# Turning all attention probabilities on VectorE in 32 by 32 blocks, with value products over 32 rows

## What is computed

```python
sc = einsum('bqkgd,bckd->bqkgc', qg, kv_c[:, :, 0]) * scale       # compressed blocks: 32 means of 32 keys
pc = masked_softmax(sc, mc);  o_c = einsum('bqkgc,bckd->bqkgd', pc, kv_c[:, :, 1])
...                                                               # top 16 of 16 blocks of 64: all causal keys
ps = masked_softmax(ss, ms);  o_s = einsum('bqkgns,bqknsd->bqkgd', ps, g[..., 1, :])
sw = einsum('bqkgd,blkd->bqkgl', qg, kv_w[:, :, 0]) * scale       # window: the last 512 keys
pw = masked_softmax(sw, mw);  o_w = einsum('bqkgl,blkd->bqkgd', pw, kv_w[:, :, 1])

o = sum(sigmoid(g_raw) * o_br, axis=branches)                     # layer_output
y_att = rms_norm(o * silu(z_a), att_norm_g)
mix = concatenate([y_ssd, y_att]) @ w_out
y = rms_norm(x + gate[:, None] * mix, final_g)
```

## Time and profile before

| what | us |
|---|---|
| median of three runs | 952.32 (951.27 to 952.5) |
| the profiled execution | 953.35 |
| its span, first to last instruction | 951.5 |
| TensorE busy in the span | 903.9 (95%) |
| VectorE, ScalarE, GpSimd busy | 473.2, 361.1, 148.6 |

### The profile page before, as it was taken

One profiled execution on the slowest core, in us unless ns is written; L12 is line 12 of the kernel. 1 busy time (PEld: TensorE's weight loads), 2 busy tenths in 40 slices (PEclk: granted clock), 3 DMA queues, 4 the chain that ended last, 5 costly groups with the idle time before them and its releaser, 6 DMA issues.

```text
span 951.5 us, 13061 instructions
## 1 busy us (share of the span) xinstructions
PE 903.9 (95%) x5085; PEld 546.6 (57%) x5085; DVE 473.2 (50%) x951; ACT 361.1 (38%) x731; POOL 148.6 (16%) x128
## 2 busy tenths in 40 slices
PE   2999999999999999998999997899999999999995
PEld 1454664465566556666455554566766665756752
DVE  1142211055353535448434458877675766658553
ACT  3040000201011244555233347666564655454531
POOL 1002583002000143335111103600000000000000
PEclk9999999999999999999999999899999999999999
DMA  8916335223120000304433304300010110101011
GB/s 295 381 54 271 133 132 207 87 89 134 43 90 1 0 5 1 89 0 156 166 137 137 137 5 154 130 1 23 2 35 1 46 33 12 46 1 45 13 34 66
DMA packets 36567, 80.72 MB, mean 85 GB/s; under 512 B 3044, under 2 KB 17580, under 8 KB 35162
## 3 DMA queue, kind: packets, MB, share of 16 engines
q1 hardware_dynamic: 32010, 49.45, 15.1%
q0 software_dynamic: 4496, 30.44, 8.4%
HBM read 69.70 MB, written 14.30 MB: 88 GB/s over the span
## 4 chain that ended last, share of the span: by engine, by line
PE 89%; DVE 5%; ACT 2%; issue 2%; DMA 1%; SPq 1%; DVEq 0%; ACTq 0%
PE PS L1692 12%; PE PS L1622 12%; PE PS L1965 12%; PE PS L1672 11%; PE PS L2024 7%; PE PS L2001 6%; PE PS L2048 6%; PE PS L1591 3%; PE PS L1781 2%; PE PS L1541 1%; PE PS L1916 1%; DMA W<-in_w_ada 1%; PE PS L1844 1%; PE PS L1626 1%; PE PS L2042 1%
## 5 line engine op out<-in xcount | busy, mean ns | idle before, releaser
L1692 PE MATMUL PS<-hT,W 128*128 128x363 f32 (+1 forms) x384 | 118.6, 469 | 0.0
L1672 PE MATMUL PS<-W,hT 128*128 128x512 f32 x256 | 113.0, 594 | 0.5 <-DVE W L1327 0.5
L1046 ACT ACTIVATE T<-PS,small 128x640 f32<-128x640 f32 (+7 forms) x128 | 88.7, 705 | 46.1 <-DVE small L1482 44.2
L1692 PEld LDWEIGHTS PS<-hT,W 128*128 128x128 f32 x384 | 72.2, 189 | 45.6 <-issue 1.7
L1482 DVE TENSOR_REDUCE small<-PS 128x1 f32<-128x640 f32 (+7 forms) x86 | 82.5, 971 | 28.4 <-PE PS L2015 27.7
L1622 PE MATMUL PS<-W,hT 128*128 128x288 f32 (+1 forms) x256 | 86.5, 500 | 0.0
L2024 PE MATMUL PS<-consts,T 128*128 128x128 f32 x544 | 80.8, 279 | 3.3 <-DVE U L1522 1.6
L2024 PEld LDWEIGHTS PS<-consts,T 128*128 128x128 f32 x544 | 61.9, 142 | 37.7 <-issue 31.0
L1672 PEld LDWEIGHTS PS<-W,hT 128*128 128x128 f32 x256 | 47.9, 190 | 56.3 <-issue 54.8
L1622 PEld LDWEIGHTS PS<-W,hT 128*128 128x128 f32 x256 | 48.5, 190 | 37.4 <-issue 30.7
L1965 PE MATMUL PS<-U,Y 128*128 128x512 f32 x128 | 60.0, 597 | 2.4 <-DVE Q L1502 1.3
(11 more groups left out here) (430 smaller groups left out, 1500.3 us busy)
## 6 DMA issues: line engine op xcount, KB each, us to landing
W<-in_w_in SPq DMA_DIRECT2D x5, 2048.0 KB, 8.6
W<-in_w_ada SPq DMA_DIRECT2D x8, 1024.0 KB, 10.0
U<-in_x_prompt SPq DMA_DIRECT2D x8, 512.0 KB, 7.5
W<-in_w_ada SPq DMA_DIRECT2D x2, 2048.0 KB, 7.8
U<-in_state_win_kv POOLq DMA_DIRECT2D x8, 512.0 KB
hT<-in_x_prompt SPq DMA_DIRECT2D x8, 512.0 KB, 3.9
out_y_prompt<-hT SPq DMA_DIRECT2D x8, 512.0 KB, 3.0
out_new_win_sample<-in_state_win_kv POOLq DMA_DIRECT2D x1, 4032.0 KB, 22.9
```

The costliest lines, as they stand in the source:

```text
L1046: ins = act.activation(Pb[u % 4][:, m * step:m * step + n * P], S[:, m, :], ACT.Exp, bias=sneg_m[u % 2][:, m:m + 1], accum_out=dsum[i % 2] ...
L1672: ins = nc.tensor.matmul(bank(z_bank(u)), hT3[:, k, i * P:(i + 1) * P], w, start=(k == 0), stop=(k == KT8 - 1))
L1692: ins = nc.tensor.matmul(bank(b, 0, n), w[:, k, ct % 4 * P:ct % 4 * P + P], hT3[:, k, a:a + n], start=(k == 0), stop=(k == KT8 - 1))
```

## The change

Probabilities are no longer turned on TensorE. ScalarE writes the exponents of a branch for all eight heads whole, the selected branch's in hT (hT3), the window's in T. VectorE then turns each block of 32 x 32 where it is (nc.vector.transpose, steps TURNP and CT; in the program's list STREAM_TRANSPOSE). After that a partition group of 32 rows, j, holds 32 keys (block b of a key tile) for the 32 queries 32j to 32j + 31. So the products go over 32 rows: for each key tile, block b, group j and KV head one matmul with K = 32 and M = 64, on 4 heads x 32 queries = 128 columns (step PV). Group j writes bank 4 + j, the KV head is the column half. The values must stand in each of the four partition groups: SP loads them four times from DRAM (VREP; v_dram holds the window's), tiles 0 to 4 before the attention, 5 to 7 during it into places that have come free. COPY gathers the four banks. The c branch does the same (CV): 32 matmuls a tile with K = 32 and M = 32, on 64 columns, all in one bank.

Around it the following moves: the banks 4 to 7 are handed out by tables (BANK, FREE, EMPTY), so OUT takes any of them; gate_p is multiplied into w_out by GpSimd (WGATE) once OUT 0 is done, and RES becomes one add; GpSimd takes the adds of BACK, the gate's product of GATE and that with final_g; ScalarE takes the scalings of SCALE and FINAL and all copies of queries; the c branch's mask is a table; the SSD rows of the tiles 2 to 7 are parked in DRAM (y_dram) and fetched again; x rows are loaded once the store from their place has landed. ORDER is written anew.

```diff
+        PROB = {"s": hT3[:, :, 0:SEQ], "w": T[:, 0:5 * 1024].rearrange("p (h s) -> p h s", h=AH)}
+        C = KcTs[:, 0:AH * NCB]
+        VREP = {("s", 0): Vs[:, 0:512], ("s", 1): Vs[:, 512:1024], ("w", 0): Vw[:, 0:512], ("w", 1): Vw[:, 512:1024],
+                ("s", 5): hst[:, :], ("s", 6): cmpm[:, 0:512], ("s", 7): Y3[:, TT, :]}
+        VREP |= {(k, 2 + n // 2): Y3[:, 2 + n, :] for n, k in enumerate("swswsw")}
+        VREP |= {("w", t): VREP["w", t - 5] for t in range(5, TT)}
...
-            "pttpvvvvpvvcorkoogooaruoofoonrohooofrnhf")
+            "scxodxkossdoafxdxuytossdxodxowssdtoxdorxssdodtnxxtossdodxorsxmsgrdxattdxvctftkuvckngoaooooorouooronhoooofofrorn"
...
             for k in (2, 3, 4, 5, 6, 7, 0, 1):
...
                 nc.gpsimd.tensor_scalar(wo[:, k, :], wo[:, k, :], mixgT[:, k:k + 1], None, ALU.mult).then_inc(s_wo_scaled, 1)
+            for what, u in STEPS:
+                if what == "WGATE":
+                    if u == 0:
+                        pool.wait_ge(s_gates_in, 64)
+                        pool.wait_ge(s_out, 2)
+                        pool.wait_ge(s_wo_scaled, 8)
+                    w = wo[:, u, :].rearrange("p (n c) -> p n c", n=4)
+                    nc.gpsimd.tensor_tensor(w, w, gate_p, ALU.mult).then_inc(s_wo_scaled, 1)
+                if what == "BACK":
...
+                    nc.gpsimd.tensor_tensor(Q3[:, i, :], Q3[:, i, :], spare, ALU.add).then_inc(s_added, 1)
+                if what == "GATE" and u:
...
+                    nc.gpsimd.tensor_tensor(Q3[:, tile, :], Q3[:, tile, :], za[tile], ALU.mult).then_inc(s_zmul, 1)
+                if what == "SQUARE":
...
+                    nc.gpsimd.tensor_tensor(x, x, fin_g[0:rows(MIX[u])].rearrange("p (h c) -> p h c", h=2), ALU.mult).then_inc(s_added, 1)
...
+                        if i:
+                            act.wait_ge(s_values, 2 * i - (1 if k == "s" else 0))
...
+                            ins = act.activation(PROB[k][:, hh, 0:n * P], S[:, m, :], ACT.Exp, bias=sneg_m[u % 2][:, m:m + 1],
+                                                 accum_out=dsum[i % 2][:, " sw".index(k), hh:hh + 1])
...
-                    act.activation(OT, bank(6), ACT.Copy).then_inc(s_copied, 1)
+                    act.activation(OT.rearrange("p (g a q) -> p a g q", g=GQ, a=4), PS[:, 4 * 512:].rearrange("p (a s) -> p a s", a=4)[:, :, 0:P]
+                                   .rearrange("p a (g q) -> p a g q", g=GQ), ACT.Copy).then_inc(s_copied, 1)
...
-                    nc.vector.tensor_tensor(x, bank(7) if u else bank(7)[SR * again:SR * again + SR], gate_p[:, c] if u else gate_s[again],
-                                            ALU.mult).then_inc(s_gated, 1)
...
-                    nc.vector.tensor_tensor(x, x, xre[u % 2][0:r, again, :], ALU.add).then_inc(s_summed, 1)
+                        nc.vector.tensor_tensor(x, use_bank("OUT", u, again), x, ALU.add).then_inc(s_summed, 1)
...
+                if what == "TURNP":
+                    us = TURNS[u]
+                    i, k, _, nh = UNITS[us[0]]
+                    n = keys(us[0])[1]
+                    dve.wait_ge(s_exp, us[-1] + 1)
+                    for hs in turn_heads(us):
+                        x = PROB[k][:, hs, 0:n * P]
+                        ins = nc.vector.transpose(x, x)
+                    ins.then_inc(s_pturned, 1)
...
-                    for n, (unit, c) in enumerate(x for b in bl for x in b[3]):
-                        ins = nc.tensor.transpose(bank(4 + F % 2, n * P, (n + 1) * P), Pb[unit % 4][:, c:c + P], ident)
+                elif what == "CV":
+                    pe.wait_ge(s_pturned, TURNED["CT", u])
+                    bank_free("CV", u, 0)
+                    for h in range(AH):
+                        for j in range(4):
+                            q, a = slice(32 * j, 32 * j + 32), h // GQ * 256 + j * HD
+                            ins = nc.tensor.matmul(use_bank("CV", u, 0)[q, h * HD:(h + 1) * HD], C[q, 32 * h:32 * h + 32], Vbd[q, a:a + HD],
+                                                   start=True, stop=True)
+                    ins.then_inc(s_cv, 1)
+                elif what == "PV":
+                    i, k = u // 2, "sw"[u % 2]
+                    a = max(0, i - WIN // P) if k == "w" else 0
+                    pe.wait_ge(s_pturned, TURNED["TURNP", LAST_TURN[i, k]])
+                    if k == "s":
+                        pe.wait_ge(kvin[i % 2], 16 + 16 * 8 * (i // 2 + 1))
+                    bank_free("PV", u, 0)
+                    for t in range(a, i + 1):
+                        for b in range(4):
+                            for j in range(4):
+                                q, c = slice(32 * j, 32 * j + 32), (t - a) * P + 32 * b
+                                for kv in range(KVH):
+                                    ins = nc.tensor.matmul(bank(4 + j, 0, P)[HALF[kv]].rearrange("p (g q) -> p g q", g=GQ),
+                                                           VREP[k, t][q, b * P + kv * HD:b * P + kv * HD + HD],
+                                                           PROB[k][q, kv * GQ:kv * GQ + GQ, c:c + 32],
+                                                           start=(t == a and b == 0), stop=(t == i and b == 3))
                     ins.then_inc(s_values, 1)
...
+            def load_values(t):
...
+                for k, rows_of in (("s", O["new_slc_prompt"][0, 0, t * P:(t + 1) * P, 1].rearrange("s h d -> s (h d)")), ("w", v_dram[t * P:(t + 1) * P])):
+                    for j in range(4):
+                        sp.dma_start(VREP[k, t][32 * j:32 * j + 32].rearrange("p (b c) -> p b c", b=4),
+                                     rows_of.rearrange("(b p) c -> p b c", b=4)).then_inc(kvin[t % 2], 16)
...
             for n, tile in enumerate(MIX):
-                sp.wait_ge(s_squared, n + 1)
+                if 5 <= n + 3 < TT:
+                    sp.wait_ge(s_values, 2 * (n + 2) + 2)
+                    load_values(n + 3)
```

More of the change, by code:

```diff
@@ L133, in constants, with build_layer @@
     return out, np.ascontiguousarray(np.concatenate(list(parts.values()), axis=1).astype(f))
[L136 removed]
+def build_layer(nc, A, O, where, ncols, gate_dram, out_dram, y_dram, v_dram):
     ctx = ExitStack()
@@ L388, in build_layer @@
         gate_rows = Y[0:9, 3328:4352]
+        WLOADS = [sum(len(GROUPS[n]) for n in range(len(GROUPS)) if SLOT[n] == x) for x in range(2)]
         def arrived(eng, g):
@@ L637, in emptying @@
-        def emptying(what, u):
-            return FILLS["T", u] if what == "EMPTY" else FILLS.get((what, u), []) if what != "T" else []
-        def turn_parts(what, u, n):
-            b = bank(4 + emptying(what, u)[n] % 2)
-            if what == "TURN":
-                return [(mixT(MIX[u], n), b[:, 0:4 * rows(MIX[u])])]
-            cols = P * sum(len(bl[3]) for bl in TGROUPS[u][1])
-            return [(PT[u % NPT][:, 0:cols], b[:, 0:cols])]
-        def q_bank(u):
-            return bank(4 + FILLS["QT", u][0] % 2) if u else bank(6)
@@ L654, in build_layer @@
-        xre = [hT3[:, 2 * n:2 * n + 2, 512:1024] for n in range(2)]
-        res = [hT3[:, 4 + 2 * n:6 + 2 * n, 512:1024] for n in range(2)]
-        gate_p, fin_g = W[:, 0:DM], W[:, DM:2 * DM]
+        POS = {(what, u, again): n for n, ((what, u), again) in enumerate(zip(STEPS, AGAIN))}
+        ROOTED = {step: n + 1 for n, step in enumerate(step for step in STEPS if step[0] in ("SCALE", "FINAL"))}
+        ADDED = {step: n + 1 for n, step in enumerate(step for step in STEPS if step[0] in ("BACK", "SQUARE"))}
@@ new lines, in use_bank, with square_junk @@
+        def use_bank(*use):
+            return bank(BANK[use])
+        def q_bank(u):
+            return use_bank("QT", u, 0) if u else bank(6)
+        xrows = [W[:, (1 + n) * DM:(2 + n) * DM] for n in range(2)]
+        xres = [x.rearrange("p (h c) -> p h c", h=2) for x in xrows]
+        gate_p, fin_g = hT3[:, 0:4, 768:1024], W[:, 0:DM]
+        def square_junk(u):
+            return hT3[:, 4:8, 768:1024] if u <= 3 else W[:, 4096 + 512 * (u - 2):5120 + 512 * (u - 2)].rearrange("p (n c) -> p n c", n=4)
```

415 lines of the change are left out of this document (206 added, 209 removed).

## The result

The changed kernel takes 966.0 us (median of four runs, 961.3 to 972.4), against 951.8 for the kernel before: 1.015 of its time, with a 95% interval of 1.009 to 1.022. It is slower, by 14 us, where I had forecast 54 us less. Its runs also lie further apart than those of before (951.1 to 952.5). The profiled execution is 961.28 us, the fastest of the four, and its span is 959.5.

A forecast was written before the change was run, and what follows sets the result against it. From OUT 0 on TensorE was taken as the bound: 611.5 to OUT 0, 251.5 of TensorE work, 18 for VectorE, 3 for GpSimd, 4 for value loads and 9.3 of tail made a span of 897.3; forecast 898 us, range 874 to 955.

The forecast's parts named there:

- The values: Value products on TensorE behind OUT 0: eight tiles at once, 13.6 ns a record, 56.6 us for 57.7, 1.1 off.
- The transposes: TensorE's turns of probabilities: all 544 records go, 70.3 us off behind OUT 0.
- OUT 0: Stretch before OUT 0: it begins at 611.5 us instead of 616.3, 4.8 off, held by the scaling of w_out.
- VectorE: VectorE's work from 568 us on becomes 225 us; TensorE waits 18 us for it, from 5 to 40.
- GpSimd's w_out product: GpSimd multiplies gate_p into w_out behind OUT 0, 18.8 us; OUT 1 waits 3 us, from 0 to 8.
- Value loads: SP's fetches of values for tiles 5 to 7 during attention: 4 us of waiting, from 0 to 12.
- The tail: Work after the last matmul: 9.3 us for 8.0, from 7.5 to 10.5.
- (1): Value products: only four tiles run at once, 27 ns a record; 942 us, from 930 to 955; chance 0.14.
- (3): VectorE's transposes take two passes, 72 us more, and VectorE bounds the phase; 925 us; chance 0.10.
- (4): The c products, four row groups writing one bank, run one after another, 27 us for 7; 918 us; chance 0.05.
- (2): TensorE's instructions come too slowly for the products; gain used up at 14.7 ns each, 996 us at 20; chance 0.15.

The follow-up runs named there:

- The experiment: The kernel before, with each transpose of probabilities made twice, 544 records more: 1006.6 us, 54.0 more.
- quarter_values: The changed kernel with only the first 32 keys of each key tile in the value products, 528 matmuls for 2112: 909.6 us.
- early_adds: The changed kernel with the two adds of BACK of tile 0 made by VectorE again, not GpSimd: 954.8 us, 1.0004 of before.
- one_head: The changed kernel with most 32-row products on one head's 32 columns instead of four heads' 128, same number of instructions: 989.1 us.
- merged37: early_adds with some 40% of the 32-row products of both KV heads merged, in branches of three and more key tiles: 963.5 us.
- merged_first_a: early_adds with merged products for both KV heads, all of a branch's merged ones first and then the others: 953.3 us.

## Why the prediction was wrong

The sum was 897.3 us for the span, and the profiled span is 959.5. Of the 62 us, 15 lie before OUT 0 and 48 behind it; the tail gives 1 back. (The median of the runs lies 5 us above the profiled one.)

**The values.** The pace was right: 14 ns a record, eight tiles at once. The rule of 25 ns between starts of the Trainium skill ("TensorE: Matmul & The Clock Gate", Part 1, "Wait — 56ns, not 53.3ns?") doesn't hold between different tiles here, by the same 14 ns. What failed is that I made the supply of instructions a rival that decides all or nothing, with a break-even at 14.7 ns an instruction and 0.15 for it, and put it at nothing in the sum. It was there at 13.5 to 14.6 ns (256 in 3.45 to 3.73 us), half as fast as the products ask: 29 us of idle time behind OUT 0, and some 6 us more in the streams. The rival's own formula would have said so: at 13.5 ns it gives 898 + 57 - 13 = 942. I worked out a packet each 1.7 us from the earlier trace rows, and had no row that said a packet could come that often.

**The transposes.** This term was mis-sized: I took 70.3 us off, and 56.7 went, since the busy time of a group isn't its share of the time. The experiment gave 99 ns a record, where I took 145; by it only 48 us went. The same that I used for the pace of 0.43 us had the time from start to start: eight turns begin at 884.36 and the next work at 885.32, 120 ns each.

**OUT 0.** It began at 626.3 us, 14.8 later than the 611.5 of the sum. The step said that nothing else before 616.3 changes on TensorE's path. I had GpSimd's new adds down as "covered by OUT and scores" and priced them, but didn't place them in GpSimd's queue, where the order shows them behind L848 (the rows L848, L865 stand in the section on the change). So I priced the adds and missed that the first ones stand behind 23 us of other work.

**VectorE.** The transposes in blocks took what the nearest row said, 128 x 2048 in 2293 ns, and VectorE's whole work from 568 us on was 231.9 us, where I had 225.

```profile
L1550 DVE STREAM_TRANSPOSE hT<-hT 128x2048 f32<-128x2048 f32 x4 | 9.2, 2293 | 0.0
```

The shortage was over-sized: I had 18 us for it, and all waits for other engines behind OUT 0 rose by 12. I take it that the slower TensorE gave VectorE time. With the still shorter products of quarter_values the waits for ScalarE's exponents rose by 14 us; what they would be with all products at full pace no run shows.

**GpSimd's w_out product** took 2485 ns each, for 2350 in L705's row, and TensorE did not stand still for it, where I had put 3 us. **Value loads** cost nothing visible, where I had put 4 us. **The tail** is 8.7 us, near the 9.3 of the sum.

**The rivals.** (1), four tiles at once, and (3), two passes, are out. (4) is out: a tile's c products span 1.0 us, though four row groups write one bank.

```profile
879.05 1.10 PE L2069 MATMUL PS<-Vbd,KcTs 32*32 32x64 f32 x64
880.07 0.53 PE L2048 MATMUL PS<-KTw,W 64*128 64x320 f32 x1
```

The Trainium skill ("TensorEngine Tiling (Array Packing)", Gotcha 1) says that different row tiles can't access the same PSUM bank at one time. The trace doesn't agree: the 64 records take 16 ns each with the array's depth, where one after another they would take 53. (2) was the right mechanism with a wrong size, and alone it wouldn't have made the kernel slower: without GpSimd's queue the change is a draw. In the long run the draw has a simple sum, an estimate from these rows. A key tile costs 128 instructions, 1.73 us at 13.5 ns each. Before, it cost 8 turns of 99 ns and 16 records of 56 ns, 1.69 us.

**Still open:** why a fetch starts some 1 us after a resumption and is usable 1.3 to 1.6 us after it has landed; why scores between the products made the kernel slower; and the spread of the runs (961 to 972 us). The mean clock of its four runs is 0.972 to 0.981, the highest in the fastest, and 0.989 before. Only one of the four has a trace, in which the granted clock is at 0.5 in the wait before OUT 0, from 603 to 620 us, and again from 838 to 841, behind pauses; in early_adds stretches of the second kind stand elsewhere, at 777, 900 and 910 us.

## What to carry to other kernels

Count instructions, not only columns: where one large matmul becomes four small ones that run side by side, the stream of instructions can be the bound. If no row shows a rate that the plan needs, put a price for it into the sum. Price a removed group by its pitch, start to start, not by its busy time. When work goes to an idle engine, write down what stands ahead of it in that engine's queue at that time, and what waits behind it.

## What the runs showed of the hardware

- Eight tiles of 32 x 64 run at once, each record of 128 columns 14 ns behind the last; with 32 columns, the first 124 records of a branch took 11 ns each.
- TensorE's instructions come in packets of 256. Where they were used up faster than they came, TensorE stood still at the end of a packet, and from one such pause to the next it was mostly 3.45 to 3.73 us (up to 4.0 in one_head), 13.5 to 14.6 ns an instruction (after, early_adds and one_head, streams of 128 and 32 columns).
- From a matmul over 128 columns of the array to one over 64 it took 304 ns from start to start (merged37, merged_first_a), and 198 ns the other way (merged37).
- With a quarter of the columns and the same number of instructions the granted clock was lower, 0.921 for 0.981, and the kernel 23 us slower (one_head).
